# One layer stage of a hybrid encoder: the next pair's strict scores ahead of the outputs, copies on ScalarE, masks and products on GpSimd, and the head norm inside the next inversion

## The reference, cut to what matters

```
def step(S, inp):
    r_t, w_t, k_t, v_t, a_t, b_t = inp
    sa = einsum("dbhij,dbhj->dbhi", S, a_t)
    S = S * w_t[..., None, :] + sa[..., :, None] * b_t[..., None, :] + v_t[..., :, None] * k_t[..., None, :]
    return S, einsum("dbhij,dbhj->dbhi", S, r_t)
...
y = ys forward + ys backward
y = ((y - mean) * rsqrt(var + eps)) * ln_g + ln_b
bonus = (sum(r * kd * r_k))[..., None] * v
return (y + bonus) * g
```

## Time and profile before

| | |
|---|---|
| median of 3 runs (lowest, highest) | 3622.22 us (3599.12, 3625.92) |
| profiled execution, own time | 3605.71 us |
| its span | 3604.0 us |
| granted TensorE clock, mean | 0.947 |
| TensorE busy | 3306.6 us (92%) |
| VectorE busy | 2227.8 us (62%) |
| ScalarE busy | 1622.0 us (45%) |
| GpSimd busy | 437.0 us (12%) |
| HBM read | 472.47 MB, 132 GB/s |

### The profile page before, as it was taken

The page is one execution under the profiler, slowest core; times in us unless marked ns, Lnnn a source line. Parts: engine busy times, 40 slices in busy tenths (PEclk is TensorE's granted clock), DMA queues, the critical chain, the costliest instruction groups (busy, mean ns, idle before and its releaser), DMA issues.

```text
span 3604.0 us, 55774 instructions
## 1 busy us (share of the span) xinstructions
PE 3306.6 (92%) x19450; PEld 2923.3 (81%) x19450; DVE 2227.8 (62%) x3615; ACT 1622.0 (45%) x2429; POOL 437.0 (12%) x263
## 2 busy tenths in 40 slices
PE   6999778888899999999989997788889999999998
PEld 6999667777788888887789996787777888888876
DVE  4565666567677777544455655656776777775444
ACT  5444323344555555444354443233445555554443
POOL 2000000244022222100000000002440222220000
PEclk9999788799899999999999997888999999999999
DMA  5566000111466666555555660001115666656554
GB/s 173 155 175 186 22 0 0 52 53 48 124 192 186 186 190 195 188 187 177 165 158 162 181 174 1 0 1 58 48 47 160 190 189 189 187 182 199 187 194 134
DMA packets 263066, 477.13 MB, mean 132 GB/s; under 512 B 16988, under 2 KB 80280, under 8 KB 261720
## 3 DMA queue, kind: packets, MB, share of 16 engines
q1 hardware_dynamic: 262872, 474.63, 43.0%
HBM read 472.47 MB, written 2.10 MB: 132 GB/s over the span
## 4 chain that ended last, share of the span: by engine, by line
PE 76%; DVE 12%; issue 4%; ACT 3%; DVEq 3%; DMA 1%; POOL 1%; ACTq 0%; POOLq 0%; SPq 0%
PE ps L505 75%; DVE Z L1405 1%; DVE scores L1663 1%; DVE wlo L1382 1%; PE ps L509 1%; DVE XS L1438 1%; DMA ring<-in_w_ple_gate_dram 1%; ACT whi L1016 1%; ACT L1016 1%; DVE scores L1814 0%; DVEq L1407 0%; DMA ring<-in_w_in_dram 0%; ACT Z L1016 0%; POOL wlo L441 0%; DVE heads L1467 0%
## 5 line engine op out<-in xcount | busy, mean ns | idle before, releaser
L1382 DVE TENSOR_TENSOR wlo<-ring,whi 128x1024 fp32r<-128x1024 f32 (+4 forms) x902 | 1130.5, 1267 | 835.0 <-ACT whi L1016 833.2
L505 PE MATMUL ps<-upair,whi 128*128 128x512 f32 (+1 forms) x5248 | 1421.5, 342 | 19.8 <-DVE wlo L1382 17.9
L1016 ACT ACTIVATE whi<-ring 128x1024 fp32r<-128x1024 f32 (+4 forms) x944 | 943.7, 1004 | 1049.9 <-PE ps L505 969.2
L505 PE MATMUL ps<-upair,wlo 128*128 128x256 f32 x4032 | 1134.9, 281 | 0.0
L505 PEld LDWEIGHTS ps<-upair,whi 128*128 128x128 f32 x5248 | 910.4, 190 | 138.6 <-DVE wlo L1382 20.3
L505 PEld LDWEIGHTS ps<-upair,wlo 128*128 128x128 f32 x4032 | 768.2, 191 | 0.0
L505 PE MATMUL ps<-whi,upair 128*128 128x390 f32 (+2 forms) x1280 | 362.7, 362 | 2.0 <-DVE wlo L1382 2.0
L505 PE MATMUL ps<-whi,ghi 128*128 128x512 f32 x704 | 278.5, 396 | 2.3 <-DVE wlo L1382 2.3
L505 PE MATMUL ps<-whi,glo 128*128 128x512 f32 x704 | 277.8, 395 | 0.0
L505 PE MATMUL ps<-wlo,ghi 128*128 128x512 f32 x704 | 277.7, 395 | 0.0
L505 PEld LDWEIGHTS ps<-whi,upair 128*128 128x128 f32 x1280 | 237.2, 188 | 24.3 <-DVE wlo L1382 3.2
(11 more groups left out here) (282 smaller groups left out, 3690.2 us busy)
## 6 DMA issues: line engine op xcount, KB each, us to landing
ring<-in_w_up_dram SPq DMA_DIRECT2D x352, 512.0 KB, 3.9
ring<-in_w_down_dram SPq DMA_DIRECT2D x176, 512.0 KB, 4.5
ring<-in_w_in_dram SPq DMA_DIRECT2D x128, 384.0 KB, 3.6
ring<-in_w_out_dram SPq DMA_DIRECT2D x64, 512.0 KB, 3.8
ring<-in_w_ple_gate_dram SPq DMA_DIRECT2D x64, 512.0 KB, 4.5
ring<-in_w_in_dram SPq DMA_DIRECT2D x64, 390.0 KB, 3.2
ring<-in_w_in_dram SPq DMA_DIRECT2D x48, 512.0 KB, 4.4
ring<-in_w_in_dram SPq DMA_DIRECT2D x32, 396.0 KB, 4.0
```

What stands on the lines that cost most here:

```text
L505: return pe.matmul(o_, a, b, start=start, stop=stop, skip_group_check=True)
L1016: return act.activation(o_, i_, f, **kw)
L1382: v.tensor_tensor(wlo[:, slot % RING, :, 0:w], ring[:, slot % RING, :, 0:w], whi[:, slot % RING, :, 0:w].bitcast(F32), SUB).then_inc(S["lo ...
```

## The change

- **Scores in two parts.** The strict b scores (kind 2) of the next pair are made in the tail, ahead of the outputs (`rw_strict`, eight products of 128 columns), into banks 0, 1, 4 and 5. The key scores (eight of 256 columns) follow when the sum of the directions is taken (`rw_yc`), the b scores with r (eight of 128) come behind level 0, the turned keys behind level 1, the first values behind level 4.
- **Masks.** VectorE masks only kind 2, with two COPY_PREDICATED of 256 elements for each direction. ScalarE copies the other kinds from PSUM to SBUF, and GpSimd masks them there with selects (two of 1024 elements and two of 512 a pair).
- **Head norm.** The variance of a pair comes behind the start of the next inversion, the scaling, gating and the bonus behind its level 0. The same four operations and waits follow the last pair.
- **Preparation.** The squares, the factor of the keys, r times `r_k`, and the copy of `KBt` move from VectorE to ScalarE; the products KB, the coefficient sum and AR move to GpSimd (`rw_products`). VectorE keeps the decays, behind levels 1 and 2, without the copy. AR and Vt have two buffers; the odd AR lies in the fourth slot of `ring`.
- All four pairs are written out instead of looped. The gate sums use bank 5 instead of 7. The memsets of `scores` go.

```diff
+                def rw_products(c):
+                    pool.wait_ge(S["rw_rn"], n + 1)
+                    pool.tensor_tensor(ch[:, 4, :], ch[:, 1, :], ch[:, 3, :], ALU.mult)
+                    pool.drain()
+                    for d in range(2):
+                        pool.tensor_tensor(KB[d][:, 0, :], ch[:, 5 - 5 * d, :], k_, ALU.mult)
+                        pool.tensor_tensor(KB[d][:, 1, :], ch[:, 4, :], swa[:, 1, d, c, :], ALU.mult)
+                    pool.drain()
+                    pool.tensor_tensor(ch[:, 3, :], KB[0][:, 0, :], KB[1][:, 0, :], ALU.add)
+                    pool.drain()
+                    pool.tensor_tensor(ch[:, 3, :], ch[:, 3, :], ch[:, 2, :], ALU.mult).then_inc(S["rw_cf"], 1)
+                    for d in range(2):
+                        pool.wait_ge(S["rw_exp"], n2 + (d + 1))
+                        pool.tensor_tensor(KB[d][:, :, :], KB[d][:, :, :], bmid(ew[d][:, 1, :], 2), ALU.mult)
+                        pool.tensor_tensor(ARC[c % 2][d][:, :, 0, :], third(ch[:, 4, :], 2), third(ew[d][:, 2, :], 2), ALU.mult)
+                        pool.tensor_tensor(ARC[c % 2][d][:, :, 1, :], third(r_, 2), third(ew[d][:, 0, :], 2), ALU.mult)
+                        pool.drain().then_inc(S["rw_ops"], 1)
+                def rw_masks(c):
+                    for i, (k0, nk) in enumerate(((0, 2), (3, 1))):
+                        for d in range(2):
+                            pool.wait_ge(S["rw_scc"], n6 + (2 * i + d + 1))
+                            sel(part, part, ALU.is_ge, -1 if nk > 1 else 0, pattern, cm)
+                            pool.drain().then_inc(S["rw_masked"], 1)
...
+            def rw_strict(c, n2):
+                for d in range(2):
+                    pe.wait_ge(S["rw_ops"], n2 + (d + 1))
+                            last = mm(ps[4 * d + h][:, t * P:(t + 1) * P], KB[d][hp, 1, t * P:(t + 1) * P],
+                                      ARC[c % 2][d][hp, t, 0, :], True, True)
+                    last.then_inc(S["rw_nt"], 1)
...
+                    pe.wait_ge(S["rw_coefc"], n + 1)
+                    if c:
+                        pe.wait_ge(S["rw_yc"], n)
+                    rw_scores(c)
+                    hooks = {0: output_scores, 1: keys_turned, 4: early_values}
+                    hooks[2 if more else 3] = next_norms if more else gate_sums
+                    invert(m2, lambda d, j: scores[d][:, 2, j, :], hooks,
+                           {(0, "t", d): lambda d=d: pe.wait_ge(S["rw_scc"], n6 + (d + 1)) for d in range(2)})
...
+                    for d in range(2):
+                        pe.wait_ge(S["rw_uf2"], n2 + (d + 1))
                     if more:
+                        rw_coefficients(n + 1)
+                        rw_strict(c + 1, pe.snap(n2 + 2))
+                    pe.wait_ge(S["rw_masked"], n4 + 4)
...
+                    for d in range(2):
+                        act.wait_ge(S["rw_sc"], n6 + (d + 1))
+                        for h in (1, 0):
+                            last = a(scores[d][:, 0:2, 2 * h:2 * h + 2, :],
+                                     ps[4 * d + 2 + h][:, :].rearrange("p (t k c) -> p k t c", t=2, k=2), ACT.Copy)
+                        last.then_inc(S["rw_scc"], 1)
+                    if c:
+                        rw_rstd(n - 1)
...
+                        if more and lv == 2:
+                            rw_norms(c + 1, n + 1)
+                        if more and lv in (2, 3):
+                            rw_decays(c + 1, n2 + 2, lv - 2)
...
+                def rw_pair(c, more):
+                    for d in range(2):
+                        v.wait_ge(S["rw_nt"], n2 + (d + 1))
+                        v.tensor_copy(st[:, 3, d:d + 1], ps[4 * d][:, 0:1])
+                        for h in range(2):
+                            v.copy_predicated(mono(scores[d][:, 2, 2 * h:2 * h + 2, :]),
+                                              mono(pred[d][:, 2 * h:2 * h + 2, :]).bitcast(I16), ps[4 * d + h][:, 0:T])
+                        invert_start(d, scores[d][:, 2, :, :])
+                    if c:
+                        rw_variance()
+                    def between_levels(lv):
+                        if lv == 0:
+                            if c:
+                                rw_out(c - 1, n - 1)
+                            rw_bonus(c, n)
+                        if more and lv in (1, 2):
+                            rw_decays(c + 1, lv - 1)
+                        if lv == 4:
+                            for d in range(2):
+                                v.wait_ge(S["rw_pv"], n2 + (d + 1))
+                                v.tensor_copy(rf[d][:, 0, :], ps[4 * d + 3][:, 0:P]).then_inc(S["rw_rf"], 1)
```

More of the change, by code:

```diff
@@ L438, in split_lo @@
+                pool.wait_ge(S["lora_ready"], L * 8 + 8)
+                rw_products(0)
+                for c in range(RC):
+                    rw_masks(c)
+                    if c < RC - 1:
+                        rw_products(c + 1)
                 def split_lo(at_slot, slot):
@@ L564, in invert, with rw_scores @@
+            def rw_scores(c):
+                for d in range(2):
+                    for h in range(2):
+                        for t in range(NT):
+                            hp = slice(64 * h, 64 * h + 64)
+                            last = mm(ps[4 * d + 2 + h][:, t * T:(t + 1) * T], KB[d][hp, 0, t * P:(t + 1) * P],
+                                      ARC[c % 2][d][hp, t, :, :], True, True)
+                    last.then_inc(S["rw_sc"], 1)
             def invert(m2, nt, between=None, inside=None):
@@ L705, in rw_pair, with output_scores @@
-                    invert(m2, lambda d, j: scores[d][:, j, 2, :],
-                           {1: lambda: rw_prepare(c + 1, n + 1, 0), 5: lambda: rw_prepare(c + 1, n + 1, 1)} if more
-                           else {3: gate_sums})
+                    if c:
+                        pe.wait_ge(S["rw_yc"], n)
+                    rw_scores(c)
+                    def output_scores():
+                        for d in range(2):
+                            for h in range(2):
+                                for t in range(NT):
+                                    hp = slice(64 * h, 64 * h + 64)
+                                    last = mm(ps[4 * d + 1 + 2 * h][:, T * (1 - h) + t * P:T * (1 - h) + (t + 1) * P], KB[d][hp, 1, t * P:(t + 1) * P],
+                                              ar[d][hp, t, 1, :], True, True)
+                            last.then_inc(S["rw_sc"], 1)
@@ new lines, in keys_turned, with next_norms @@
+                    def keys_turned():
+                        for d in range(2):
+                            pe.wait_ge(S["rw_scc"], n6 + (d + 3))
+                            F = FIRST[d]
+                            for j in range(2):
+                                last = turn(ps[4 * d + 3][:, T + j * P:T + (j + 1) * P], KB[d][:, j, F * P:(F + 1) * P])
+                            last.then_inc(S["rw_sc"], 1)
+                    def next_norms():
+                        pe.wait_ge(S["rw_scc"], n6 + 6)
+                        rw_norms(c + 1, n + 1)
@@ new lines, in early_values @@
+                    def early_values():
+                        pe.wait_ge(S["rw_scc"], n6 + 6)
+                        pe.wait_ge(S["rw_vtc"], n + 1)
+                        pe.wait_ge(S["rw_masked"], n4 + 2)
+                        if more:
+                            pe.wait_ge(S["rw_rn"], n + 2)
+                            pe.wait_ge(S["rw_vtc"], n + 2)
+                        for d in range(2):
+                            F = FIRST[d]
+                            for h in range(2):
+                                last = mm(ps[4 * d + 3][:, 64 * h:64 * h + 64], scores[d][:, 0, 2 * h + F, :],
+                                          vt[:, F, 64 * h:64 * h + 64], True, True)
+                            last.then_inc(S["rw_pv"], 1)
@@ L715, in rw_pair @@
                         last.then_inc(S["rw_u"], 1)
+                    if not more:
+                        pe.wait_ge(S["gd_cumc"], L + 1)
                     for d in range(2):
@@ L1715, in _ @@
                 v.wait_ge(S["gate_ready"], L + 1)
                 v.wait_ge(S["mixp_in"], L * MIXP_TOTAL + MIXP_TOTAL)
-                for stage in range(6):
-                    rw_prepare(0, v.snap(L * RC), stage)
+                for d in range(2):
+                    rw_decays(0, d)
                 rw_coefficients(v.snap(L * RC))
-                rw_operands(0, v.snap(L * RC))
-                v.drain()
-                with v.Fori(0, RC - 1) as c:
-                    rw_pair(c, True)
@@ L1724, in _ @@
-                rw_pair(RC - 1, False)
+                for c in range(RC):
+                    rw_pair(c, c < RC - 1)
+                rw_variance()
+                rw_out(RC - 1, v.snap(L * RC + (RC - 1)))
                 v.memset(V1[:, :, :, P:P + 1], 1.0)
```

334 lines of the change are left out of this document (159 added, 175 removed).

## The result

The changed kernel takes 3563.11 us (median of 4 runs, 3550.0 to 3570.83) where the kernel before, beside it, takes 3618.72 us (4 runs, 3599.12 to 3625.92): a ratio of 0.986, 95% interval 0.983 to 0.989, or 38 to 63 us less. A second measurement of the same kernel gave 0.983 (0.979 to 0.988). The forecast was 3572 us.

What follows compares the result with a forecast made beforehand. No engine is full; the pair is a chain between engines, open at VectorE's handover. Gains of 2.3 + 8.3 + 8.3 + 6.3 = 25.2 us a layer, 50 in both, gave 3572 us; range 3535 to 3606.

Steps and rivals of the forecast that it cites:

- The handover: From the sum of both directions to the first level-1 XS: 24.5 us becomes 16.0, gain 8.5 us each, three a layer.
- The port term: In the handover, GpSimd's masks hold up VectorE's two-input products: 0.5 + 1.2 us added, between nothing and 7.5.
- the other terms: Handover steps from masks through variance and level 0 to scaling and gating, without the held port: 14.1 us.
- The selects: GpSimd's masks in the handover, taken as 1.1 and 0.6 us each, 2.5 for 1024 elements at the two-input rate.
- Rival 1: Held port: slow selects or VectorE's products waiting cost up to 5.8 us more a handover, 35 in all; chance 22%.
- Level 1 to level 4: Inversion levels: gain 0.5 us from copies leaving levels 1 to 3, and 3.4 from level 3 to level 4.
- Level 4 to the sum: End of a pair: losses of 0.7 us (ScalarE's copy late), 1.3 (first values uncovered) and 2.1 (strict scores ahead of outputs).
- the coefficients: Move from level 5 to the tail of a pair, claimed to cost nothing.
- The rest of a pair: Everything in a pair outside the handover, gains and losses together: net -0.2 us.
- rival 2: Shrinking gaps bring TensorE's clock from 1.2 to 2.4 GHz: 24 us more gain, 37 at most; chance 20%.
- GpSimd's products: Thirteen operations beside the inversion, 11.7 us with drains, end before they are needed: no cost, cover 3.7 us.
- The ends: First and last pair of a layer: gains of 2.3 us (first XS 3.7 earlier, less 1.2 and 0.2) and 6.3 us.

Runs made afterwards that it cites:

- Late masks: Changed kernel with GpSimd's masks waiting until VectorE has written XS of level 0 or 1; 3542.85 us (0.980 of before), again 3550.79 us (0.984).
- the gaps filled: Changed kernel plus TensorE products nobody reads, where it waits for copies inside the inversion of every pair; 3556.56 us, 0.983 of before.
- lengthening: Changed kernel with 14 more GpSimd products of 256 elements in front of every pair's chain; 3624.8 us, 1.001 of before.
- the unrolled one: Kernel before with only its loops over a layer's first three pairs written out on every engine; 3618.43 us, 1.000 of before.

## Why the prediction was right, point by point

- **The handover, 24.5 to 16.0 us.** Measured 15.9 in the second pair, and 14.6 and 17.0 in the others of the first trace. *The port term was mis-sized*: it was taken as 1.7 us, and what the held instructions lost is 0.7 us in the second pair (1.15 for 0.69 and 0.70 for 0.42) and 1.2 in the third (1.34 for 0.43 and 0.69 for 0.42). Late masks, at 14.0, still holds one for 0.6 us, so the handover without any hold is some 13.4 us, where the other terms sum to 14.1. That 15.9 agrees with 16.0 is chance: 1.7 us of it is level 0 at half clock (from its first XS to level 1 it takes 8.29 us in the second pair and 6.55 in the third).
- **The selects.** Taken as 1.1 and 0.6 us, with 2.5 as the bound. They take 1.09 and 0.64, the latter where nothing disturbs it, and 0.90 beside VectorE's scaling. Rival 1 (22%) had its rows, come again at 465.84 and 527.83, but a handover holds two products, one of them for 0.3 us only.
- **Level 1 to level 4.** 19.8, 19.5 and 18.3 us in the first three pairs before, 15.6 in all of those after. Only the 18.3 is at full clock (row below), so 2.7 us is what the order gives; the steps had 0.5 + 3.4 = 3.9. The 3.4 was mis-sized because level 3 was read at 8.0 us in the first pair, where the clock was down (0.79); at full clock it takes 6.5, and 4.0 after.
- **Level 4 to the sum.** 16.75 us before at full clock; with the new order 19.9 at full clock (late masks, 489.25 to 509.14). The loss is 3.1 us, where the steps had 0.7 + 1.3 + 2.1 = 4.1. ScalarE's wait is 0.3 and the first values 1.0 us. The strict scores take 1.26 us (from 456.84) and not the 2.1 of the same number of products in a level, and the coefficients, put at nothing, take some 0.5 in the tail.

```profile
550.19:568.51 18.32, 12.87 (x104) 11.81 (x102) 14.54 (x36) 8.32 (x15) 0.00 (x0) 1.00 0.00 0
444.96:461.71 16.75, 15.87 (x140) 14.86 (x140) 6.75 (x16) 5.69 (x15) 0.00 (x0) 1.00 0.01 2
```

- **So a pair at full clock** is 24.5 + 18.3 + 16.75 = 59.6 us before and 14.6 + 15.6 + 19.9 = 50.1 after (neither handover is wholly at full clock in these traces, 0.79 and 0.85): 9.5 us of gain, against the 8.3 of the forecast for the second and third pair. The rest of a pair comes to 2.7 - 3.1 = -0.4, where the forecast had -0.2, two errors of 1 us that cancel; the excess is the handover's. In the traces a pair gained 3.8 and 8.6, in layer two 1.8 and 8.6.
- **The clock** is what the steps left out, and rival 2 (20%), which had it, had the wrong sign: shorter gaps were to bring the clock up and give 24 to 37 us more. The granted clock over the stage is 0.80 and 0.79 in the two layers before, 0.81 and 0.82 after, and 0.79 and 0.81 in the second trace. Against the pair at full clock the middle pairs of layer one lost 3.9 and 1.8 us before, and 9.6 and 2.7 after. Before, about half of the second pair's time at 1.2 GHz lay in the handover (472.1 to 482.4), much of it where TensorE waited for VectorE anyway:

```profile
472.00:478.00 6.00, 1.65 (x7) 1.25 (x7) 5.74 (x11) 0.00 (x0) 0.00 (x0) 0.51 0.00 0
```

  After the change most of it lies in the tail, where TensorE is the path: the tail, from the first product with rf to the sum, takes 11.1 us at 2.4 GHz (498.0 to 509.1 in the full pair of late masks) and 19.4 at 1.2 (499.7 to 519.1 with the gaps filled; the tail has nothing added there). These 8 us are about the size of the difference between the pairs of 59.7 and of 52.8 us (6.9, of which 5.6 lie from level 4 to the sum and 1.3 in the handover), and they took back what the handover gave beyond the forecast.
- **GpSimd's products.** Cover 3.7 us forecast, 7.8 read and 6 measured by lengthening. A pair's thirteen take 10.8 us with their drains (402.74 to 413.56 in the first pair) where the forecast had 11.7. The two-input rate is as in the earlier trace rows (1267 and 726 ns beside 1274 and 738):

```profile
L458 POOL TENSOR_TENSOR KB<-KB,YB 128x512 f32<-128x512 f32 x8 | 10.1, 1267 | 1.0 <-issue 1.0
L402 POOL TENSOR_SCALAR_AFFINE_SELECT scores<-scores 128x1024 f32<-128x1024 f32 x8 | 8.7, 1091 | 0.0
L402 POOL TENSOR_SCALAR_AFFINE_SELECT scores<-scores 128x512 f32<-128x512 f32 x8 | 6.7, 834 | 0.0
L450 POOL TENSOR_TENSOR KB<-YB,Z 128x256 f32<-128x256 f32 x8 | 5.8, 726 | 0.6
```

- **The ends.** First pair: first XS 23.9 us behind the copy of sgate, against 29.0 before; the gain is 5.1 where 3.7 was forecast, and the pair's 3.1 and 5.4 (2.3 forecast). Last pair: 5.5 and 5.7 (6.3 forecast).
- **The sum.** The stages give 42 us by the first trace and 38 by the second, both against one trace of the kernel before (against the unrolled one, 36 and 31), where the forecast had 50. The time shows 51 by the ratio, with 38 to 63 as its interval. The forecast's mechanism and range hold. That the median came within 9 us is in part luck: the stage fell 8 to 12 us short, which the readings above lay to the clock, and the time does not show it. That the remainder is noise of the rest of the span (3077 to 3101 us) is read from the table, not shown by an experiment.

What stays open: what makes the clock fall in the last level and the tail, and what sets how long it stays down. It fell there with and without gaps. In the kernel after it stays down for 24 us in one middle pair and 7 in the next, with the same instructions, and late masks has pairs with no fall at all.

## What to carry to other kernels

When a wait ahead of an engine goes, ask which clock the work behind it runs at: time at half clock under a wait cost nothing here, and the same work on the path took 8 us more. Work handed to an idle engine has a price at both ends, as the slack of the engine that feeds it (here ScalarE's, which was zero) and the cover of what it makes (6 to 8 us here), and both can be measured by lengthening it. An edit of 10 us in a kernel of 3600 doesn't show in the time; measure the stage in the trace, more than once where the clock moves in it (here it varied by 5 to 8 us), and say that it is the stage.

## What was not expected of the hardware

- A select on GpSimd with one input in SBUF holds a VectorE product of two SBUF inputs just as a GpSimd product does: 1.15 us instead of 0.69, and 1.34 instead of 0.43. It works the other way too: a select of 512 elements takes 0.90 us beside VectorE's scaling and 0.64 where it runs alone (below). The Trainium skill, "SBUF — State Buffer", section "Who interferes with whom", has it so (a VectorE instruction with two SBUF inputs contends with a GpSimd instruction that reads SBUF, and whichever starts first keeps the pair to its end); the trace agrees. Reductions and transposes beside a select kept their time (0.42 and 0.71 us).
- TensorE's granted clock fell from 2.4 to 1.2 GHz behind 11 us without a gap, and stayed there for 24 us at a busy share of 0.9 and more (with the gaps filled, 499.4 to 523.3). With the same instructions the stay was 7 us in another pair of the changed kernel.

The select of 512 elements in the timeline of the kernel after, beside the scaling:

```profile
476.62 0.90 POOL L402 TENSOR_SCALAR_AFFINE_SELECT scores<-scores 128x512 f32<-128x512 f32 x1
```

The same select in the second trace of late masks:

```profile
475.17 0.64 POOL L402 TENSOR_SCALAR_AFFINE_SELECT scores<-scores 128x512 f32<-128x512 f32 x1
```

The elements and the pattern are the same, so GpSimd is held by VectorE as VectorE is by GpSimd, 0.26 us here.
